# Norms in a streamed-weight transformer: three weight slots by token tile around each norm instead of two, transposes ahead of the last, and norms that end in halves

## The reference

```
for l in (0, 1):                       # first kind: norm before the layer
    h = rms_norm(x, attn_norm_g[l])    # x * rsqrt(mean(x*x) + eps) * g
    z = h @ w_in[l]                    # q, k, v of two attentions, two gates
    ...                                # window attention (rope), neighbourhood attention
    x = x + mixed @ w_out[l]
    h = rms_norm(x, ffn_norm_g[l])
    x = x + (silu(h @ w_gate[l]) * (h @ w_up[l])) @ w_down[l]
for l in (0, 1):                       # second kind: norm after the layer
    x = layer_norm(ALPHA * x + token_mixer(x), g, b)      # (x - mean) * rsqrt(var + eps) * g + b
    y = swiglu(x) if l == 0 else moe_ffn(x)               # 8 experts, top 2, hidden 3584
    x = layer_norm(ALPHA * x + y, g, b)
```

## Time and profile before

| | |
|---|---|
| median of 3 runs | 2497.27 us (2496.53 to 2497.75) |
| profiled execution | 2498.05 us, span 2496.7 us |
| TensorE busy | 2371.1 us (95% of the span) |
| VectorE busy | 1742.2 us (70%) |
| ScalarE busy | 1375.2 us (55%) |
| GpSimd busy | 68.6 us (3%) |
| weights and other reads | 577.42 MB, 232 GB/s over the span |
| experts, 1500 to 2470 us | TensorE busy 970.0 of 970 us, loads at 335 to 359 GB/s |

### The profile page before, as it was taken

The page is one execution under the profiler, slowest core; times in us unless marked ns, Lnnn a source line. Parts: engine busy times, 40 slices in busy tenths (PEclk is TensorE's granted clock), DMA queues, the critical chain, the costliest instruction groups (busy, mean ns, idle before and its releaser), DMA issues.

```text
span 2496.7 us, 31183 instructions
## 1 busy us (share of the span) xinstructions
PE 2371.1 (95%) x12708; PEld 2049.2 (82%) x12708; DVE 1742.2 (70%) x2209; ACT 1375.2 (55%) x1781; POOL 68.6 (3%) x91
## 2 busy tenths in 40 slices
PE   6999999989999998899999879999999999999997
PEld 5788887789788898788799868888888888888885
DVE  5646555656554455745555668998989898999997
ACT  4443443444444343344344327777777777777774
POOL 3200001200000000000000000000000000000000
PEclk9989999999999998899999979999999999999998
DMA  7216554524554422555442356999999989999994
GB/s 237 102 68 228 185 191 127 188 85 158 188 186 169 169 82 102 219 191 197 145 162 96 119 219 269 371 350 364 354 363 354 365 350 368 354 361 354 367 356 188
DMA packets 93734, 580.58 MB, mean 233 GB/s; under 512 B 21728, under 2 KB 22928, under 8 KB 24336
## 3 DMA queue, kind: packets, MB, share of 16 engines
q1 hardware_dynamic: 91728, 571.61, 61.1%
q10 hardware_dynamic: 1856, 6.91, 0.8%
HBM read 577.42 MB, written 1.06 MB: 232 GB/s over the span
## 4 chain that ended last, share of the span: by engine, by line
PE 71%; DVE 6%; ACT 2%; issue 1%; POOL 0%; DVEq 0%; ACTq 0%
PE bank L435 22%; PE bank L437 21%; PE bank L436 21%; PE bank L432 5%; DVE wl L1311 2%; PE bank L581 1%; ACT L L1014 1%; DVE L L1538 1%; ACT wh L950 1%; DVE X L1396 0%; DVE HL L1326 0%; POOL SM L1944 0%; DVE U L1672 0%; PE bank L617 0%; DVE SM L1342 0%
## 5 line engine op out<-in xcount | busy, mean ns | idle before, releaser
L1311 DVE TENSOR_TENSOR wl<-raw,wh 128x1024 fp32r<-128x1024 f32 x706 | 830.5, 1224 | 208.8 <-ACT wh L950 207.3
L950 ACT ACTIVATE wh<-raw 128x1024 fp32r<-128x1024 f32 x706 | 707.0, 1054 | 317.9 <-PE bank L437 304.9
L435 PE MATMUL bank<-wh,GH 128*128 128x512 f32 x896 | 351.9, 393 | 0.0
L437 PE MATMUL bank<-wh,GL 128*128 128x512 f32 x896 | 349.7, 390 | 0.0
L436 PE MATMUL bank<-wl,GH 128*128 128x512 f32 x896 | 349.4, 390 | 0.0
L1311 DVE TENSOR_TENSOR wl<-spare,wh 128x1024 fp32r<-128x1024 f32 x264 | 310.0, 1221 | 22.9 <-ACT wh L950 22.5
L435 PE MATMUL bank<-wh,HH 128*128 128x512 f32 (+1 forms) x768 | 292.3, 381 | 33.0 <-DVE HL L1326 21.3
L435 PE MATMUL bank<-HH,wh 128*128 128x256 f32 x1024 | 300.1, 293 | 13.1 <-DVE HL L1326 7.6
L950 ACT ACTIVATE wh<-spare 128x1024 fp32r<-128x1024 f32 x264 | 264.8, 1055 | 64.6 <-PE bank L437 64.6
L436 PE MATMUL bank<-HL,wh 128*128 128x256 f32 x1024 | 295.9, 289 | 0.0
L437 PE MATMUL bank<-HH,wl 128*128 128x256 f32 x1024 | 295.4, 289 | 0.0
(11 more groups left out here) (228 smaller groups left out, 3211.6 us busy)
## 6 DMA issues: line engine op xcount, KB each, us to landing
raw<-in_ws SPq DMA_DIRECT2D x353, 1024.0 KB, 5.3
spare<-in_ws SPq DMA_DIRECT2D x132, 1024.0 KB, 6.1
more<-in_ws SPq DMA_DIRECT2D x48, 1024.0 KB, 4.8
once<-in_ws SPq DMA_DIRECT2D x4, 1024.0 KB, 7.9
QT<-in_relb SPq DMA_DIRECT2D x4, 768.0 KB, 14.3
LNB<-in_ln ACTq DMA_DIRECT2D x3, 1024.0 KB, 4.6
raw<-in_ws SPq DMA_DIRECT2D x2, 816.0 KB, 4.5
LNB<-in_ln ACTq DMA_DIRECT2D x3, 512.0 KB, 3.7
```

The costliest lines, as they stand in the source:

```text
L435: T.q.matmul(o, l[0], r[0], start=start, stop=False)
L437: return T.q.matmul(o, l[1], r[0], start=False, stop=stop)
L950: A.q.activation(sets[c % NSET][0][:, half * i:half * i + half], raws[stream.place[n]][:, half * i:half * i + half], ACT.Copy).then_inc(*h ...
L1311: V.q.tensor_tensor(wl[:, half * i:half * i + half], raw[:, half * i:half * i + half], wh[:, half * i:half * i + half].bitcast(f32), ALU.s ...
```

## The change

TensorE: the product ahead of a norm takes its last three slots by tile, and tile 0's transposes stand ahead of the last slot-tile of tile 1. After the norm a third slot is taken by tile too: `gu` of a feed-forward (its first half), kva in blocks of the first kind; in blocks of the second kind nothing is added (`third` does nothing). Each group of four transposes waits for its own half of the normed tile. ScalarE and VectorE: the split of the next layer's first slot moves behind tile 0's norm, its turned copy ahead of the second slot's split. The RMS norm multiplies by the gain first, beside ScalarE's square, then by the root in two halves; the layer norm becomes (x - mean) * gain, issued ahead of the wait for the root, then * root + bias in two halves. In block l = 0 the splits of slots 3 and 4 and both kva copies stand ahead of the sines and the rope angles. The square's scratch output is another buffer. The output leaves in four transfers of half a tile instead of two. Waits for a normed tile elsewhere name its second half.

```diff
-    if b == 4:
-        for h in range(2):
-            T.wait_ge(*out("dn", 1, t, h))
-    else:
-        T.wait_ge(*normed.at(b, t))
     for c4 in range(2):
+        if b == 4:
+            T.wait_ge(*out("dn", 1, t, c4))
+        else:
+            T.wait_ge(*normed.at(b, t, c4))
         room = groups.take(T, "h", b, t, c4)
...
+def t_rows(room, s, t, lhs, ready, n, k0, step_k):
+    w = weights(s, step_k, 1, n)
+    for k in range(step_k):
+        t_weights(s, k)
+        T.wait_ge(*ready(k0 + k, t))
+        ins = t_mm3(room[:, 0:n], [v[:, k0 + k, 128 * t:128 * t + 128] for v in lhs],
+                    [v[:, k, 0, :] for v in w], k0 + k == 0, k0 + k == 7)
+    return ins
...
-def t_first_products(s, b, n, keys, between):
+def t_first_products(s, b, n, keys, between, third):
+    def ready(k, t):
+        return out("h", b, t, k // 4)
     for t in range(2):
         room = groups.take(T, *keys[t])
...
+        ins = t_rows(room, s, t, HV, ready, n, 0, 4)
+        if t == 1:
+            ins.then_inc(*used.mark(s))
+        t_rows(room, s + 1, t, HV, ready, n, 4, 4).then_inc(*groups.fill(*keys[t]))
         if t == 0:
             between()
+        third(t, ready)
...
-    straight = kts - 4 if tail else kts
+    straight = kts - 6 if tail else kts
...
-            for k0 in (kts - 4, kts - 2):
+            for k0 in range(kts - 6, kts, 2):
...
-                if t == 1 and k0 == kts - 4:
+                if t == 1 and k0 < kts - 2:
                     ins.then_inc(*used.mark(s_))
                     t_free(s_, used.at(s_))
+                if t == 1 and k0 == kts - 4:
+                    tail()
         t_free(s_, full(name, i, 1, 1))
-        tail()
...
+        if first and c == 0:
+            rooms = {}
+
+            def third(t, ready):
+                rooms[t] = groups.take(T, "gu", i, 0, t)
+                ins = t_rows(rooms[t], s + 2, t, HV, ready, n, 0, 4)
+                if t == 1:
+                    ins.then_inc(*used.mark(s + 2))
+            t_first_products(s, 2 * i + 1, n, [("gg", i, 0, t) for t in range(2)], first, third)
+            t_free(s + 2, used.at(s + 2))
+            for t in range(2):
+                t_rows(rooms[t], s + 3, t, HV, ready, n, 4, 4).then_inc(*groups.fill("gu", i, 0, t))
+            t_free(s + 3, full("gu", i, 0, 1))
+            s += 4
+        else:
+            for a in ("gg", "gu"):
+                t_tokens(s, lhs, ready, n, [(a, i, c, t) for t in range(tiles)])
                 s += 1 if n <= 256 else 2
         turn()
...
+
+    def kva(t, ready):
+        room = groups.take(T, "kva", l, t)
+        t_rows(room, s + KVA, t, HV, ready, 256, 0, 8).then_inc(*groups.fill("kva", l, t))
+    t_first_products(s + QA, 2 * l, 512, [("qa", l, t) for t in range(2)], lambda: t_turn_x(2 * l, 1), kva)
+    t_free(s + KVA, full("kva", l, 1))
...
-    t_tokens(s + KVA, HV, t_normed(l), 256, [("kva", l, t) for t in range(2)])
...
-    t_first_products(s + V2, 2 * l, 512, [("v", l, t) for t in range(2)], lambda: t_turn_x(2 * l, 1))
+    t_first_products(s + V2, 2 * l, 512, [("v", l, t) for t in range(2)], lambda: t_turn_x(2 * l, 1),
+                     lambda t, ready: None)
...
-        A.q.activation(LB[0][:, 1024 * t:1024 * t + 1024], XV[:, t, :], ACT.Square,
+        A.q.activation(LB[1][:, 0:1024], XV[:, t, :], ACT.Square,
...
 def a_down(s, slots, b, after_first=None):
-    for i in range(slots - 1):
+    for i in range(slots - 2):
         a_hi(s + i + 2)
         if i == 0 and after_first:
             after_first()
     a_square(b, 0)
+    a_hi(s + slots)
+    a_turn_x(b, 0)
     a_hi(s + slots + 1)
-    a_turn_x(b, 0)
     a_square(b, 1)
...
                 a_hi(s + 2)
                 first()
-                s += 2
+                s += 3
+                a_hi(s + 1)
+                a_hi(s + 2)
+                s += 1
+            elif first and c == 0:
+                continue
...
     a_copy(QAT[0][:, 0:512], ("qa", l, 0), 512)
+    a_copy(QAT[0][:, 512:768], ("kva", l, 0), 256)
+    a_hi(s + KVA + 2)
...
     if l == 0:
...
-    a_hi(s + KVA + 2)
-    a_copy(QAT[0][:, 512:768], ("kva", l, 0), 256)
     a_hi(s + QB + 2)
...
+    V.wait_ge(*ln_in.at(b))
+    V.q.scalar_tensor_tensor(xt, xt, ag[:, 0:1], gb[:, 0:1024], ALU.subtract, ALU.mult).then_inc(*step.mark())
+    V.wait_ge(*step.now())
     V.wait_ge(*root.at(b, t))
-    V.q.tensor_scalar(xt, xt, ag[:, 0:1], rs[:, 0:1], ALU.subtract, ALU.mult).then_inc(*step.mark())
-    V.wait_ge(*step.now())
-    V.wait_ge(*ln_in.at(b))
-    V.q.tensor_tensor(xt, xt, gb[:, 0:1024], ALU.mult).then_inc(*step.mark())
-    V.wait_ge(*step.now())
-    V.q.tensor_tensor(xt, xt, gb[:, 1024:2048], ALU.add).then_inc(*normed.mark(b, t))
+    for h in range(2):
+        c = slice(512 * h, 512 * h + 512)
+        V.q.scalar_tensor_tensor(xt[:, c], xt[:, c], rs[:, 0:1], gb[:, 1024 + 512 * h:1536 + 512 * h],
+                                 ALU.mult, ALU.add).then_inc(*normed.mark(b, t, h))
 
 def v_norm(b, t):
     if b < 4:
+        hv = LB[0][:, 1024 * t:1024 * t + 1024]
+        if b == 0:
+            V.wait_ge(*x_in[t].at())
+        else:
+            for h in range(2):
+                V.wait_ge(*(out("wo", b // 2, t, h) if b % 2 else out("dn", b // 2 - 1, t, h)))
+        V.wait_ge(*(g_in if b else g_first).at(b))
+        V.q.tensor_tensor(hv, XV[:, t, :], GR, ALU.mult).then_inc(*step.mark())
         V.wait_ge(*square.at(b, t))
         V.q.tensor_scalar(sm[f"ms{t}"], sm[f"ss{t}"], 1.0 / 1024, EPS, ALU.mult,
                           ALU.add).then_inc(*mean.mark(b, t))
+        V.wait_ge(*step.now())
         V.wait_ge(*root.at(b, t))
-        V.wait_ge(*(g_in if b else g_first).at(b))
-        V.q.scalar_tensor_tensor(LB[0][:, 1024 * t:1024 * t + 1024], XV[:, t, :], sm[f"rs{t}"][:, 0:1], GR,
-                                 ALU.mult, ALU.mult).then_inc(*normed.mark(b, t))
+        for h in range(2):
+            V.q.tensor_scalar(hv[:, 512 * h:512 * h + 512], hv[:, 512 * h:512 * h + 512], sm[f"rs{t}"][:, 0:1],
+                              None, ALU.mult).then_inc(*normed.mark(b, t, h))
...
 def v_down(s, slots, b, name, l, scale, after_first=None):
-    for i in range(slots - 1):
+    for i in range(slots - 2):
         v_lo(s + i + 2)
         if i == 0 and after_first:
             after_first()
     v_add_x(name, l, 0, scale)
     v_norm(b, 0)
+    v_lo(s + slots)
+    v_turn_x(b, 0)
     v_lo(s + slots + 1)
     v_add_x(name, l, 1, scale)
-    v_turn_x(b, 0)
     v_norm(b, 1)
...
                 v_lo(s + 2)
                 first()
-                s += 2
+                s += 3
+                v_lo(s + 1)
+                v_lo(s + 2)
+                s += 1
+            elif first and c == 0:
+                continue
...
     v_lo(s + 2)
     v_turn_x(2 * l, 1)
+    v_lo(s + KVA + 1)
     v_copy(QAT[1][:, 0:512], ("qa", l, 1), 512)
+    v_lo(s + KVA + 2)
+    v_copy(QAT[1][:, 512:768], ("kva", l, 1), 256)
     if l == 0:
...
-    v_lo(s + KVA + 2)
-    v_copy(QAT[1][:, 512:768], ("kva", l, 1), 256)
     v_lo(s + QB + 2)
...
     for t in range(2):
-        S.wait_ge(*normed.at(8, t))
-        S.q.dma_start(out_d[0, 128 * t:128 * t + 128, :], XV[:, t, :]).then_inc(*final_out.mark())
+        for h in range(2):
+            S.wait_ge(*normed.at(8, t, h))
+            S.q.dma_start(out_d[0, 128 * t:128 * t + 128, 512 * h:512 * h + 512],
+                          XV[:, t, 512 * h:512 * h + 512]).then_inc(*final_out.mark())
```

More of the change, by code:

```diff
@@ L459, in t_turn_x @@
                 ins.then_inc(*groups.fill("h", b, t, c4))
-        def t_first_products(s, b, n, keys, between):
+        def t_rows(room, s, t, lhs, ready, n, k0, step_k):
[9 more added lines that the diff above has]
+                return out("h", b, t, k // 4)
             for t in range(2):
                 room = groups.take(T, *keys[t])
-                for i in range(2):
-                    w = weights(s + i, 4, 1, n)
-                    for k in range(4):
-                        t_weights(s + i, k)
-                        T.wait_ge(*out("h", b, t, i))
-                        ins = t_mm3(room[:, 0:n], [v[:, 4 * i + k, 128 * t:128 * t + 128] for v in HV],
-                                    [v[:, k, 0, :] for v in w], i + k == 0, i == 1 and k == 3)
-                    if i == 1:
-                        ins.then_inc(*groups.fill(*keys[t]))
-                    elif t == 1:
-                        ins.then_inc(*used.mark(s))
+                ins = t_rows(room, s, t, HV, ready, n, 0, 4)
+                if t == 1:
+                    ins.then_inc(*used.mark(s))
+                t_rows(room, s + 1, t, HV, ready, n, 4, 4).then_inc(*groups.fill(*keys[t]))
                 if t == 0:
                     between()
+                third(t, ready)
             t_free(s, used.at(s))
@@ L485, in t_tokens @@
             for i, k0 in enumerate(range(0, 8, step_k)):
-                w = weights(s + i, step_k, 1, n)
```

(28 more changed lines are left out.)

1 line of the change is left out of this document (removed).

## The result

The changed kernel took 2478.61 us (median of 4, 2476.40 to 2480.09) where the kernel before took 2497.05 beside it: ratio 0.9928, 95% interval 0.9916 to 0.9940, so 18.4 us faster. The forecast was 2481.1, inside 2473 to 2488; the gain was 16.2 by forecast, and the two profiled executions differ by 20.6 in their spans (2496.7 and 2476.1).

A forecast was written before the change was run, and what follows sets the result against it. TensorE, busy 95% of the span, bounds the kernel with its stops, mostly on `HL` (34.5 us). Gains of 0.5 + 8.1 + 1.8 + 2.6 + 0.2 + 1.7 + 1.3 = 16.2 us from 2497.27 give 2481.1, range 2473 to 2488.

The forecast's parts named there:

- b = 1 to 3: RMS norms: the stop behind the transposes goes, 0.35 is lost ahead of the third slot; 2.7 us each, 8.1 together.
- rival C: Third slot doesn't cover tile 1's `HL`: b = 1 to 3 gain 2.0 each, not 2.7; 2483.2, chance inside the forecast's 0.57.
- Layer norms: At b = 5 to 8, GpSimd's power waits behind VectorE's gain product, so shorter norms gain only 0.65 us per tile.
- the two bounds: Layer norm's first half ready 1.25 + 0.68 after the variance (power beside the product) or 1.25 + 0.65 + 0.68 (behind); behind chosen.
- rival A: Layer norms: power runs beside the gain product, stops stay too short to lower the clock; gain 24.2, 2473.1 us, chance 0.17.
- b = 5: Layer norm costing 7.7 us: 3.4 of standing and 1.7 of low clock would remain, a gain of 2.6.
- b = 8: Final norm, two tiles one after the other: gain 1.3 us, with the four smaller output transfers counted as nothing.
- b = 4, 6, 7: Gains of 1.8 us (tile 1's 1.07 stop stays), 0.2 (stops and low clock remain) and 1.7 (VectorE's chain at the router).
- First block: Start 1.0 later, qb 2.3 earlier, but GpSimd's later tables lengthen the vb stop to 4.5; 0.5 us gained.
- Rival B: Gain partly given back by VectorE's full list at tile 1 and GpSimd crawling through first-block tables; 2487.5 us, chance 0.2.
- D: Third slot's low part 3.5 us late at b = 1, 2, 3 and 5, clock falling there; 2502.7 us, chance 0.03.

The follow-up runs named there:

- slots alone: The changed kernel with the old norms in one piece, whole-tile waits and two output transfers; 2482.88 us.
- no third slot: The changed kernel with `third` doing nothing in any block, so kva and `gu` are taken after both tiles as before; 2493.08 us.
- the repeat: The changed kernel run again with no edit, as the measure for later edits; 2479.36 us (2477.36 to 2480.26).
- gain last: The changed kernel with the gain product of the first norm (b = 0) moved behind the root, fused with the root's product in halves; 2478.15 us.
- norms alone: The kernel before with only the shorter norms, half-wise waits and four output transfers, slot order as before; 2496.31 us, no change.
- both: The changed kernel with rope angles and sines moved earlier in the first block and the first norm's gain product behind the root; 2474.12 us.

## Why the prediction was right, and where it was off

*b = 1 to 3.* Right by its steps: no stop behind the transposes, tile 0's `HL` ready long before it is wanted, and a stop on `wl` ahead of the third slot (0.49 to 0.52, I had 0.35). 8.6 of 8.1. What I had wrong is why it works. I credited the shorter norms with being in time at tile 1; slots alone shows that without them the stop is as short, only at another place, and 2.5 of 2.9 us is gained per norm. And rival C priced a missing third slot at 0.7 per block; no third slot measured 1.75 in stops and low clock besides. The split that stands between tile 1's norm and its `HL` I had counted at b = 6 (2.45, measured 1.85 to 2.31) and left out of C.

*Layer norms.* The choice between the two bounds was right: the power is held by VectorE's product (1.52 against 0.55), and rival A is out. That is as the Trainium skill has it (SBUF — State Buffer, "Who interferes with whom"): the one of the two that comes later is blocked. The trace adds that the power ends 0.41 after the instruction that held it. Sized too dear: VectorE's idle time behind the product is 0.50 to 0.53, not 0.65. So b = 5 stood 2.40 + 0.52 where I had 2.7 + 0.7, and in the profiled pair its low clock cost 1.3 where I had 1.7 (7.7 less 3.5, less 2.9): 3.5 instead of 2.6. In the repeat the same sum gives 2.9 for the low clock and a gain of 1.9. So the stops were 0.5 shorter than forecast, and on which side of 2.6 the gain lies is the clock's doing. b = 8 was off most for the same reason and one more: the two norms took 9.57 us instead of 11.33, 1.76 less, and the tail behind the last instruction fell from 2.64 to 2.13, which I had counted as nothing. No run has the four output transfers by themselves, so that they shortened the tail is likely and not shown.

*b = 4, 6, 7.* 2.1, 0.5 and 1.5 against 1.8, 0.2 and 1.7; in the repeat 2.1, -0.4 and 2.1.

*First block.* Every event came in the order given (angles 42.00, tables 47.04, vb stop longer), but GpSimd was slow in only four of the twenty instructions, since VectorE idled between its splits, and ended at 55.7 and not at 57; VectorE went on at 57.72 where I had 59.0, and TensorE stood 3.62 where I had 4.5. The other part is the start. I had it 1.0 late; it was 1.8 late, but fewer slow first products left 0.4 of that, so qb came 3.0 earlier and not 2.3. Together 1.8 and not 0.5, of which 0.8 went again to a lower clock behind the longer stop by 113. I had seen that the gain arrives last, and priced it at 0.4 to 1.0; gain last measured 1.7 at the start and at vb.

*Clock at stops that nobody edited.* Not a term of my sum. The entries run from -2.8 to +1.6 and happened to sum to 0.2 in the profiled pair; that the total came so near the forecast is in this part luck. The median's gain of 18.4 lies 2.2 below the pair's 20.6, inside what executions of one kernel differ by.

*Rival B* (lists too full, GpSimd crawling) and *D* (the third slot's low part late by 3.5): the waits were 0.5, so neither point was reached.

## What to carry to other kernels

The shorter norms alone changed nothing that can be told from noise, the order alone was worth 14 us and both 18: before shortening a step, look at whether what waits for it is also queued behind other work of its own engine. Work moved ahead on a helper engine pushes something behind it, so the cover (here the third slot) and the move are one edit; price them together, and price leaving one out with the queue as it then stands. Leaving out the third slot was priced at 2.1 us in the prediction (rival C) and cost 14. A chain that starts with a late transfer should have all it can do ahead of the wait, and only what needs the data behind.

## What was not expected of the hardware

The stop of 2.35 to 2.37 us ahead of layer 1's V projection is untouched in all thirteen traces. Where it ended between 461.3 and 467.2 us (seven kernels) the 5 us after it had a granted clock of 1.00; where it ended between 468.9 and 472.8 (six) it was 0.66, that is, part of it at the 1.2 GHz level. Two of these windows (start and end, PE, PEld, DVE, ACT, POOL busy, clock, DMA share, GB/s), first of the changed kernel, then of no third slot:

```profile
465.94:470.94 5.00, 5.00 (x22) 4.15 (x23) 5.00 (x7) 0.00 (x0) 1.38 (x2) 1.00 0.57 179
```

```profile
471.59:476.59 5.00, 5.00 (x15) 4.00 (x16) 5.00 (x7) 0.00 (x0) 1.38 (x2) 0.66 0.53 182
```

22 matmuls against 15 in the same 5 us. The kernels of the second group are also those with a stop over 1 us at b = 1 or b = 2; whether the earlier stops or the moment decides is open. The moment alone does not decide at another place: after the stop of 2.71 that ends at 1327.42 the kernel before had 1.00, and norms alone, at 1326.76, 0.50; only one other of the thirteen (both, at 1303.64) had 1.00. Such an event is worth 1.6 to 2.8 us, which is more than several of the terms above.
